# Three places of a mixture-of-experts layer at once: x ahead of the modulation weights, filler matmuls in waits, and expert weights laid out in rows of 4 KB

## The reference, cut to what matters

```python
mod = silu(c) @ w_mod + b_mod                     # (1, 6 * D): shift, scale, gate, twice
sh_m, sc_m, g_m, sh_f, sc_f, g_f = jnp.split(mod, 6, axis=-1)
h = _rmsnorm(x, norm_mix_g) * (1.0 + sc_m) + sh_m
x = x + g_m * _sliding_window_attention(h, w_qkv, b_qkv, w_o, b_o, sinks, rel_bias)
h = _rmsnorm(x, norm_ffn_g) * (1.0 + sc_f) + sh_f
# _moe: logits = h @ w_r + b_r; the top 4 experts of each token; gates = softmax of their logits
#       expert(e): u = xb @ w_in[e] + b_in[e]; _clamped_swiglu(u) @ w_out[e] + b_out[e]
#       each token's 4 results are summed with its gates
x = x + g_f * _moe(h, router_w, router_b, moe_w_in, moe_b_in, moe_w_out, moe_b_out)
return _rmsnorm(x, final_norm_g)
```

## Time and profile before

| | us |
|---|---|
| three runs | 2042.62, 2047.72, 2052.26 (median 2047.72) |
| the profiled execution | 2050.49, of which the span from the first to the last instruction is 2049.0 |
| PE, busy in the span | 1972.3 |
| DVE, ACT, POOL, busy | 638.2, 460.7, 217.2 |
| from the start to the first K product | 45.9 |
| from there to the first attention unit | 130 |
| attention and routing, to the first expert product at 520.3 | 345 |
| 32 expert slots and the end | 1529 |

### The profile page before, as it was taken

How to read it: one execution, slowest core, us unless ns; L and a number is a source line. 1 busy time by engine, 2 the same in 40 slices (tenths; PEclk the granted TensorE clock), 3 DMA queues, 4 the chain that set the end, 5 groups by cost and what they waited for, 6 DMA issues and landing times.

```text
span 2049.0 us, 52513 instructions
## 1 busy us (share of the span) xinstructions
PE 1972.3 (96%) x23799; PEld 1776.3 (87%) x23799; DVE 638.2 (31%) x1864; ACT 460.7 (22%) x1298; POOL 217.2 (11%) x250
## 2 busy tenths in 40 slices
PE   7999999997999999999999999999999999999997
PEld 3665875554989998999999999999999999999997
DVE  2653555565242222222222222222222222222124
ACT  3202443341121202121212111111112121112212
POOL 2003000000011101101010101111111100100002
PEclk9999999997999999999999999999999999999999
DMA  9780111102987778787878787878788888989986
GB/s 358 267 182 23 42 43 72 42 32 90 371 299 273 290 269 302 275 308 287 293 282 323 270 316 281 325 287 323 285 319 310 299 302 332 324 331 331 326 317 229
DMA packets 76596, 524.04 MB, mean 256 GB/s; under 512 B 10010, under 2 KB 15794, under 8 KB 51666
## 3 DMA queue, kind: packets, MB, share of 16 engines
q1 hardware_dynamic: 57570, 467.68, 62.9%
q0 software_dynamic: 17200, 52.59, 7.5%
q10 hardware_dynamic: 1600, 0.36, 0.1%
HBM read 485.34 MB, written 34.21 MB: 254 GB/s over the span
## 4 chain that ended last, share of the span: by engine, by line
PE 93%; DVE 3%; issue 2%; ACT 1%; DMA 1%; POOL 0%; SPq 0%; DVEq 0%; ACTq 0%; POOLq 0%
PE ps L1603 46%; PE ps L1637 23%; PE ps L1464 5%; PE ps L1388 4%; PE ps L1471 3%; PE ps L1591 2%; PE ps L1577 2%; PE ps L1436 1%; PE ps L1409 1%; PE ps L1384 1%; PE ps L1421 1%; PE ps L1359 1%; PE ps L1343 1%; ACT ring L727 1%; PE ps L1328 1%
## 5 line engine op out<-in xcount | busy, mean ns | idle before, releaser
L1603 PE MATMUL ps<-U,ring 128*64 128x120 f32 (+11 forms) x13312 | 949.0, 270 | 15.3 <-issue 12.9
L1603 PEld LDWEIGHTS ps<-U,ring 128*64 128x64 f32 (+1 forms) x13312 | 929.4, 149 | 30.4 <-issue 28.9
L1637 PE MATMUL ps<-U,ring 128*64 128x120 f32 (+11 forms) x6656 | 476.2, 271 | 6.9 <-issue 6.8
L1637 PEld LDWEIGHTS ps<-U,ring 128*64 128x64 f32 (+1 forms) x6656 | 463.7, 150 | 15.5 <-issue 14.8
L1199 DVE TENSOR_SCALAR U<-ps,U 128x120 f32<-128x120 f32 (+11 forms) x256 | 90.8, 355 | 1132.8 <-PE ps L1603 1095.6
L789 ACT ACTIVATE U<-U 128x120 f32<-128x120 f32 (+11 forms) x256 | 80.2, 313 | 913.3 <-DVE U L1199 910.8
L800 ACT ACTIVATE U<-ps,U,modT 128x120 f32<-128x120 f32 (+11 forms) x256 | 118.6, 463 | 296.9 <-PE ps L1637 296.5
L554 POOL DMA_INDIRECT acc_d<-U x43 | 43.2, 1005 | 742.4 <-DVE U L1191 738.8
L1464 PE MATMUL ps<-ring 128*128 128x512 f32 x256 | 115.3, 603 | 4.7 <-DVE xr L989 4.6
L1464 PEld LDWEIGHTS ps<-ring 128*128 128x128 f32 x256 | 47.8, 192 | 63.8 <-issue 63.7
L775 ACT ACTIVATE U<-ps,modT,Af 128x120 f32<-128x120 f32 (+11 forms) x252 | 94.2, 463 | 13.1 <-PE ps L1577 11.1
(11 more groups left out here) (222 smaller groups left out, 1137.5 us busy)
## 6 DMA issues: line engine op xcount, KB each, us to landing
ring<-in_moe_w SPq DMA_DIRECT2D x191, 2048.0 KB, 9.1
U<-in_w_mod SPq DMA_DIRECT2D x8, 2048.0 KB, 10.8
ring<-in_w_mod SPq DMA_DIRECT2D x4, 2048.0 KB, 19.7
ring<-in_w_qkv SPq DMA_DIRECT2D x3, 2048.0 KB, 18.6
acc_d<-xr SPq DMA_DIRECT2D x10, 512.0 KB, 2.6
xr<-in_x SPq DMA_DIRECT2D x8, 512.0 KB, 12.8
ring<-in_w_o SPq DMA_DIRECT2D x2, 2048.0 KB, 8.6
xn_d<-U SPq DMA_DIRECT2D x8, 512.0 KB, 2.6
```

The source lines that it names most:

```text
L1603: last = pe.matmul(bank(j % 4)[lo:hi, s * 256:s * 256 + n], w[:, k, s, (j % 2) * P + lo:(j % 2) * P + hi], xT[:, k, 0:n], start=(k == 0), ...
L1637: last = pe.matmul(bank(m % 4)[lo:hi, 0:n], w[:, k, (m % 4) * P + lo:(m % 4) * P + hi], actT[:, k, 0:n], start=(k == 0), stop=(k == KT - 1))
```

## The change

1. **Front.** x tiles 0 to 3 are loaded first, then w_mod pieces 0 to 2, and piece 3 as two transfers (even and odd row blocks) into another buffer, the place of `wq`; so `wq` waits for the fourth partial product. PE transposes x tiles 0 to 3 before the modulation rounds, ACT and DVE copy them out as they are, and DVE applies `Am` and the shift afterwards in eight operations of 128x512 in SBUF. The first K product takes the slices one by one.
2. **Fillers.** Matmuls whose result nobody reads (128x128 times 128x512) stand ahead of waits: two before modulation round 2, two before the first K product (`fill_wait`), and in the routing one or two ahead of some logits, ranks and products, and one ahead of the first rows of the experts (`keep_busy`).
3. **Routing order.** The choice of the last tile is made before the list of tile 6 is added; its ranks use another PSUM bank; `in_group` is made earlier.
4. **Weights.** A piece lies in memory as [4 runs][128 partitions][4 KB] instead of [128 partitions][16 KB], and each transfer has rows of 4 KB. Of the first piece three quarters are loaded ahead of the first gather, and one quarter after it, instead of two halves.

```diff
-        stages = [U[:, 0:PIECE], U[:, PIECE:2 * PIECE], piece(5), piece(3)]
+        stages = [U[:, 0:PIECE], U[:, PIECE:2 * PIECE], piece(5), piece(0)]
...
+        def choice_bank(t):
+            return bank(0) if t == LAST else bank(3)
...
         def load_piece(eng, e, p, done):
-            eng.dma_start(piece(p), moe_w[bass.ds(e, 1), p].rearrange("o p n -> (o p) n")).then_inc(done, 16)
-        def load_half(eng, e, p, h, done):
-            part = slice(h * PIECE // 2, (h + 1) * PIECE // 2)
-            eng.dma_start(piece(p)[:, part], moe_w[bass.ds(e, 1), p, :, part].rearrange("o p n -> (o p) n")).then_inc(done, 16)
+            eng.dma_start(piece(p).rearrange("p (q n) -> p q n", q=NRUN),
+                          moe_w[bass.ds(e, 1), p].rearrange("o q p n -> (o p) q n")).then_inc(done, 16)
+        def load_runs(eng, e, p, first, end, done):
+            eng.dma_start(piece(p).rearrange("p (q n) -> p q n", q=NRUN)[:, first:end, :],
+                          moe_w[bass.ds(e, 1), p, first:end].rearrange("o q p n -> (o p) q n")).then_inc(done, 16)
...
-            for n in range(4):
-                load_mod(n)
             for t in range(4):
                 load_x(t)
+            for n in range(3):
+                load_mod(n)
+            stage3 = stages[3].rearrange("p (t n) -> p t n", t=KT)
+            for a in range(2):
+                sp.dma_start(stage3[:, a::2, :], mod_v[3][:, a::2, :]).then_inc((s_mod[3], s_mod3)[a], 16)
...
             for t in range(4, TT):
                 load_x(t)
+            sp.wait_ge(s_mpp, NPART)
             for z in range(2):
...
-                        load_half(sp, e, 0, 0, s_wl[0])
+                        load_runs(sp, e, 0, 0, 3, s_wl[0])
                         sp.wait_ge(s_g, gathers[1] * 16)
-                        load_half(sp, e, 0, 1, s_wl[0])
+                        load_runs(sp, e, 0, 3, NRUN, s_wl[0])
...
+            def tile_copy(t):
+                act.wait_ge(s_xt, 2 * t + 1)
+                act.activation(hT[:, 0:4, t * P:(t + 1) * P], bank(x_bank(t, 0)).rearrange("p (k n) -> p k n", k=4), ACT.Copy)\
+                    .then_inc(s_hta, 1)
...
-            squares(0)
-            squares(1)
-            squares(2)
-            act.wait_ge(s_coef, 1)
-            tile_evacuate(0)
-            squares(3)
-            for t in range(1, 4):
-                tile_evacuate(t)
+            for t in range(4):
+                squares(t)
+            for t in range(4):
+                tile_copy(t)
...
+            for t in range(4):
+                dve.wait_ge(s_xt, 2 * t + 2)
+                dve.tensor_copy(hT[:, 4:8, t * P:(t + 1) * P], bank(x_bank(t, 1)).rearrange("p (k n) -> p k n", k=4))\
+                    .then_inc(s_htv, 1)
             for n in range(NPART):
...
-            for t in range(4):
-                tile_out(t)
+            dve.wait_ge(s_hta, 4)
+            dve.wait_ge(s_htv, 4)
+            for k in range(KT):
+                dve.tensor_scalar(hT[:, k, 0:4 * P], hT[:, k, 0:4 * P], Am[:, k:k + 1], modT[:, k:k + 1], ALU.mult, ALU.add)\
+                    .then_inc(s_htv, 1)
...
                 if u in normed and normed[u] == LAST:
+                    link(dve.tensor_scalar(in_group, e_f[:, 0:4], float(E), p_e[:, 0:1], ALU.mult, ALU.add))
+                    link(dve.tensor_scalar(in_group, in_group, p_f[:, 0:1], None, ALU.is_equal))
                     choose(choose_at[u])
...
-                if u in place_at and place_at[u] < TT - 1:
+                if u in place_at and place_at[u] == LAST - 1:
+                    choose(LAST)
+                if u in place_at and place_at[u] < LAST:
                     add_list(place_at[u])
...
+            for t in range(4):
+                x_transpose(t)
+            def fill_wait(n):
+                for _ in range(n):
+                    pe.matmul(bank(3), ident[:, :], xr[:, 0, 0:512], start=True, stop=True)
             for n in range(NPART):
+                if n == 2:
+                    for b in (s_hta, s_htv):
+                        pe.wait_ge(b, 4)
+                    fill_wait(2)
                 mod_partials(n)
                 mod_products(n)
-            for t in range(4):
-                x_transpose(t)
+            fill_wait(2)
             pe.wait_ge(s_wkv, 16)
...
                 for k in range(KT):
+                    if n == 0:
+                        pe.wait_ge(s_htv, 4 + k + 1)
...
+            def keep_busy(n):
+                for _ in range(n):
+                    pe.matmul(bank(5), ident[:, :], U[:, 8192:8704], start=True, stop=True)
+            busy_logits = {LAST - 1: 1}
+            busy_ranks = {LAST - 2: 1, LAST - 1: 2, LAST: 2}
...
                         xn2_transpose(LAST, 1)
+                        keep_busy(2)
                         logits(LAST)
...
             last.then_inc(s_cnt, 1)
+            keep_busy(1)
             lists(TT - 1)
...
+    pieces = np.concatenate([first, second], axis=1)
+    return pieces.reshape(E, NPIECE, P, NRUN, PIECE // NRUN).transpose(0, 1, 3, 2, 4)
```

More of the change, by code:

```diff
@@ L44 @@
 NPIECE = 6
+NRUN = 4
 QUERY_HALVES = ((0, 64), (64, P))
@@ L259, in program @@
         s_sq = sem("squares_done"); s_rstd = sem("rstd_ready")
-        s_xn = sem("x_scales_ready"); s_mpp = sem("mod_partial_product"); s_xt = sem("x_transposed"); s_hta = sem("hT_by_act"); s_htv = sem("hT_by_dve")
+        s_xn = sem("x_scales_ready"); s_mpp = sem("mod_partial_product"); s_xt = sem("x_transposed"); s_hta = sem("hT_by_act"); s_htv = sem("hT_by_dve"); s_mod3 = sem("mod_piece_odd_rows_loaded")
         s_coef = sem("norm_coefs")
@@ L699, in _ @@
                 if n == 0:
+                    act.wait_ge(s_coef, 1)
                     tile_evacuate(4)
@@ L997, in norm2 @@
                     .then_inc(s_xn2, 1)
-            def logits_bank(t):
-                return bank(0) if t == LAST else bank(3)
             def choose(t):
@@ L1005, in choose @@
                     dve.wait_ge(s_router, 32)
-                link(dve.tensor_tensor(out=lg[:, :], in0=logits_bank(t)[:, 0:E], in1=brB[:, :], op=ALU.add))
+                link(dve.tensor_tensor(out=lg[:, :], in0=choice_bank(t)[:, 0:E], in1=brB[:, :], op=ALU.add))
                 link(dve.max(out=top8[:, t, :], in_=lg[:, :]))
@@ L1084, in _ @@
                     last_half()
-            link(dve.tensor_scalar(in_group, e_f[:, 0:4], float(E), p_e[:, 0:1], ALU.mult, ALU.add))
-            link(dve.tensor_scalar(in_group, in_group, p_f[:, 0:1], None, ALU.is_equal))
             dve.wait_ge(s_cnt, 1)
@@ L1340, in mod_partials @@
                 for a in range(2):
+                    if n == 3 and a:
+                        pe.wait_ge(s_mod3, 16)
                     for g in range(4):
@@ L1352, in x_transpose @@
                     pe.wait_ge(s_hta, t)
-                    pe.wait_ge(s_htv, t)
+                    pe.wait_ge(s_htv, t + KT)
                 elif t >= 2:
@@ L1500, in ranks @@
                 pe.wait_ge(s_mask, t + 1)
-                last = pe.matmul(bank(3)[:, 0:E], tri[:, :], mask[:, t % 2, :], start=True, stop=(t == 0))
+                last = pe.matmul(choice_bank(t)[:, 0:E], tri[:, :], mask[:, t % 2, :], start=True, stop=(t == 0))
                 if t:
-                    last = pe.matmul(bank(3)[:, 0:E], ones[:, :], macc[:, t - 1, :], start=False, stop=True)
+                    last = pe.matmul(choice_bank(t)[:, 0:E], ones[:, :], macc[:, t - 1, :], start=False, stop=True)
                 last.then_inc(s_rank, 1)
@@ L1711, in by_piece @@
     second = w_out.reshape(E, KT, P, 2, 512).transpose(0, 3, 2, 1, 4).reshape(E, 2, P, PIECE)
-    return np.concatenate([first, second], axis=1)
+    pieces = np.concatenate([first, second], axis=1)
+    return pieces.reshape(E, NPIECE, P, NRUN, PIECE // NRUN).transpose(0, 1, 3, 2, 4)
 def kernel(x, c, w_mod, b_mod, norm_mix_g, norm_ffn_g, attn_w_qkv, attn_b_qkv, attn_w_o, attn_b_o,
```

18 lines of the change are left out of this document (10 added, 8 removed).

## The result

The changed kernel takes 2034.28 us in the median of 7 runs (2033.13 to 2039.53), the kernel before 2048.28 in 7 (2042.43 to 2052.26). The ratio is 0.9939, with a 95% interval of 0.9925 to 0.9954: 12.5 us less (9.4 to 15.4). The profiled execution took 2033.39 us, its span is 2031.9.

The account below looks back on a forecast made before the run. The prediction took TensorE, busy 1972.3 of 2049.0 us, as the bound. Front 4, routing 5.5 and weights 7 make 16.5 off the profiled 2050.5: 2034.0, or 2031 us beside the median; range 2022 to 2044.

Parts of the forecast that it names:

- Front: Before the first K product: x loaded and transposed first lets K start earlier, 4 us gained, ends +8 and -3.
- Wq behind the fourth partial product: SP load queue: wq issued at 38 lands by 55, hidden with 18 us to spare, so it costs nothing.
- Routing: From 479 to the first expert products: fillers raise the clock, new order shortens waits; 5.5 us gained, ends 9 and -6.
- that outlast their wait (+0.9): Routing: fillers, two before logits(7) and two before ranks(7), last longer than the waits they fill, costing 0.9 us.
- a quarter needs 1.3 less: End of routing: loading a quarter of piece 0 after the gather, instead of half, saves 1.3 us.
- The 1.5 us in slot 0: First expert slot: of 1.9 us lost to the low clock in its first 62 matmuls, 1.5 come back.
- The granted clock: Sign for the routing: over 0.85 from the last two o products to the first expert product; staying at 0.6 refutes.
- Weights in rows of 4 KB: Expert slots: smaller weight packets shorten TensorE's stops for late instruction blocks, 7 us gained, ends 0 and 10.8.
- What can change is who waits behind a 16 KB packet: Expert slots: instruction blocks and gathers queue behind weight packets; by the skill page, 4 KB makes a block's wait a quarter.
- the 10.8 us: Nine TensorE stops over 0.5 us from 600 to 1700 in the old profile, the pool from which 7 us was taken.
- the stops stay: Rival, chance 0.22: in the expert slots queues turn by a piece's share, so smaller rows change nothing; 2038 us.
- Slower, by the rate of reading: Rival, chance 0.07: a partition's runs 512 KB apart lower the read rate below 280 GB/s; at 270, 2090 us.

Follow-up runs that it names:

- front_only: Only the front part of the change put on the kernel before, routing and weights as before: 2041.35 us, ratio 0.9966.
- routing_only: Only the routing's new order and its fillers put on the kernel before, piece 0 still in halves: 2044.02 us, ratio 0.9982.
- nokeep: The changed kernel without the fourteen fillers of the routing, its new order kept: 2021.66 us, ratio 0.9959 to the kernel before.
- quarter_weights: The changed kernel, but from slot 2 on each weight piece loads only its first quarter: 2003.56 us in one run.
- front_routing: The changed kernel with weights again in rows of 16 KB and piece 0 in halves: 2035.11 us, ratio 0.9940 to the kernel before.

## Why the prediction was right or wrong

The forecast was 2031 us for the kernel, from 16.5 us gained; it took 2034.28, 12.5 gained (9.4 to 15.4). The sum of the parts was right to a quarter, the parts were not: the weights fell short by 5.4 us and the front gave 3.0 more, so that the total came out so near is in part luck.

**Front: 4 us, measured 7.0 (4.7 to 9.2).** The order of the steps was right. Wkv's landing, put at 37.6, came at about 38.8 and is the floor for K in the changed kernel. Transposes from about 10, partials at 19 to 23, rounds of 3.7: found at 8.39, 18.18 and 3.78. The working took two of the four rounds at the lower level (6.3 us each) and K at 42; all four were at the higher one in the changed kernel, and K came at 38.88. Over the profiled executions K starts at 38.9, 41.5 and 41.5 with the new front on the first chips, and at 45.9, 44.1 and 42.0 with the old one: a mean gain of 3.4, near the 4. So the timed 7.0 is more than the start of K shows; its interval reaches down to 4.7, and where the rest comes from is not shown (the slots of front_only's execution are 5.5 us shorter than before's, 3.6 of them by stops, which the front doesn't touch). The fillers, which were to make one more round fast in the working, turned out to be worth nothing that can be measured.

**Wq behind the fourth partial product.** It was costed at nothing, under 18 us of cover. From K to the first scores both kernels take 129.7: right.

**Routing: 5.5 us, measured 3.7 (1.6 to 5.9).** Of the 5.5, 1.3 belong to the quarter of piece 0, which routing_only does not have, so 4.2 stand against its 3.7. The lists should come 3.8 us earlier, less 0.9 for the filler before ranks(5). Found: the ids 2.9 earlier counted from the last output product, and for that filler 0.9 by the lowest values of either kind (304.2 and 305.1, 302.7 and 303.5 or 303.6). The two steps that were too large are "that outlast their wait (+0.9)", where the second filler before ranks(7) alone cost 0.6, and "a quarter needs 1.3 less", which left out that the larger first part delays the gather: from the ids to slot 0 the changed kernel is 1.0 us faster than the kernel before and 0.7 faster than routing_only, and with 16 KB rows and three quarters ahead it is no faster (15.2). The 1.5 us in slot 0 came (43.52 us for its 256 records before, 42.36 in the changed kernel, 41.84 or 41.86 in five others), but not by fillers, as the working had it: routing_only has them and 43.4, nokeep has none and 41.84. The granted clock (over 0.85 wanted, 1.00 found) and the halves of single steps (logits 1.92 to 1.12, transposes 3.36 to 1.97) were right.

**Weights in rows of 4 KB: 7 us, measured 1.6 (-1.0 to 4.3), and 0 beside the 16 KB rows of the same kernel.** This is the term that was mis-sized; its mechanism was half right. Blocks of instructions do come late when the DMA is full: 83 of 95 stops end 1.1 to 1.8 us after a block's landing, and quarter_weights, which has the same blocks, has none of these stops. The step that failed is "What can change is who waits behind a 16 KB packet", for the blocks: packets of 4 KB leave stops of 2.05 us (7.8 us together in the mean, 8.9 with 16 KB), packets of 1 KB make more of them, and ahead of a late block the blocks start 7.3, 7.1 and 7.1 us apart with 16, 4 and 1 KB. What holds a block up, if not the packet ahead of it, stays open. Also, the 10.8 us were the stops of one execution, the highest of its layout on the first chips (7.6 to 11.3 by the count of the table), so part of the expected gain was chance. For the gathers the step held, though not to its size: beside full DMA they were to fall under 9 us, and fell from 15.0 to 10.1 in the mean, with 1 KB to 9.6. The kernel before from 690 to 730 (us to landing), and the changed kernel from 585 to 620 and from 690 to 730:

```profile
U<-xn_d,U POOLq DMA_INDIRECT x1, 14.8
```

```profile
U<-xn_d,U POOLq DMA_INDIRECT x1, 9.8
```

```profile
U<-xn_d,U POOLq DMA_INDIRECT x1, 10.4
```

The rival "the stops stay" (2038) came true for the stops; its reason, that the turn between queues is a whole piece's share, has the shorter gathers against it. The time came out between it and the forecast only because the front gave more than its term. Busy TensorE was to pass 392 of the 400 us; it was 390.11, and front_only with its old rows had 389.73.

The Trainium skill (DMA: Bandwidth & Descriptors, Queues, rings and completion order) has an engine change queues at packet boundaries. By that alone a stop would have shrunk to a quarter with 4 KB and to a sixteenth with 1 KB. The gathers, shorter by a third with 4 KB, agree with turns by packets, but the wait of a block is not set by the length of one packet: the runs show 6.2 to 11.7 us of stops at 16 KB, 6.4 to 9.9 at 4 KB and 18.9 at 1 KB.

**Slower, by the rate of reading.** The rate from 600 to 1000 is 292 GB/s after and 287 before: nothing lost. The same page (Latency and other measured facts) gives 207 GB/s for partitions at a pitch of 512 KiB; here only the four runs of one partition lie so far apart, and the rate does not fall to it.

## What to carry to other kernels

Before a term is built on stops that no semaphore explains, count them in several executions: here they varied from 6.2 to 11.7 us over six kernels with the same rows of 16 KB, and were 6.4 and 9.9 in two executions of the changed kernel, more than the rows moved. Where the loads' total sets a floor, put first in the queue what the longest work needs, and the gain is handed on; that was worth more than all the fillers, which gave 1.5 us in one place and took 0.6 to 2.6 in others, by whether the clock was up. When part of a load is pulled ahead of a gather, the gather pays for it. Shorter rows of a large load shorten the transfers beside it, and that counts only where one of them is waited for.

## What was unexpected of the hardware

**Chips differ by 1%, and so does the gain.** The kernel before took 2047.83 us on one chip and 2029.56, 2028.51 and 2028.70 on three others. The change was worth 0.61% [0.9925, 0.9954] where it takes 2048, and 0.27% [0.9962, 0.9985] on one where it takes 2029. Of the changed kernel there is a trace of each kind: up to slot 0 they take 511.5 and 511.3 us, in the slots 1520.4 and 1507.6. The chain of waits of the slower one:

```profile
787.72 0.24 issue
787.95 0.46 PE ps L1645 x6
788.42 0.29 issue
788.71 0.46 PE ps L1645 x6
789.17 1.01 issue
```

And of the same instructions on the faster one:

```profile
777.64 17.14 PE ps L1645 x448
```

On the slower chips nearly every narrow slot has short stops of some 0.25 us, in twos and threes, with six records in 0.46 us between them (448 in 17.14 are 0.038 each). Stops of 0.15 to 0.45 us come to 9.1 us in the changed kernel there and to 0.7 on the faster chip. The kernel before has 9.1 us of them too, and of the fourteen traces all six from the slower chips have 8.7 to 10.1, all eight from the faster 0.2 to 1.7: they belong to the chip and not to the change. What they wait for is open. With no trace of the kernel before on a faster chip, it is open too why the change is worth less there.

**The clock falls in one execution and not in the next.** With the same front the granted clock from 33 to 42 us was 1.00 in the changed kernel, 0.50 in front_only and 0.51 in front_routing:

```profile
33.00:42.00 9.00, 7.03 (x28) 3.17 (x29) 4.84 (x12) 1.73 (x3) 0.55 (x2) 1.00 1.04 399
```

```profile
33.00:42.00 9.00, 7.72 (x21) 3.76 (x22) 4.46 (x11) 1.88 (x3) 0.70 (x2) 0.50 1.04 400
```

TensorE had been busy for 15.33 and 15.05 of the 19 us before, nearly alike, and fillers stood in the same waits. Which of the two comes moves K's start by 2.6 us. In what TensorE did before no difference was found, so why the clock fell in one and not in the other is open.
